# Where ScalarE copies a unit's turned weights: before or behind the next unit's two exponentials

## The reference, cut to what matters

```python
def _diff_attn(q, k, v, lam):
    s = jnp.einsum("bqhcd,bkhcd->bhcqk", q, k, preferred_element_type=jnp.float32) * (ATT_QK_DIM ** -0.5)
    p = jax.nn.softmax(s, axis=-1)
    w = p[:, :, 0] - lam * p[:, :, 1]
    return jnp.einsum("bhqk,bkhd->bqhd", w.astype(v.dtype), v)

def _diff_post(o, g, lam_init):
    o = _rmsnorm(o, g, SUBLN_EPS) * (1.0 - lam_init)
    return o.reshape(o.shape[0], o.shape[1], ATT_HEADS * ATT_V_DIM)
```

## Time and profile before

| what | value |
|---|---|
| median of 3 executions | 3102.07 us (3097.54 to 3107.11) |
| the profiled execution's own time | 3098.69 us |
| its span, first to last instruction | 3097.4 us |
| mean granted TensorE clock | 0.974 of full speed |
| TensorE matmuls busy | 2915.4 us, 94% |
| VectorE busy | 1611.4 us, 52% |
| ScalarE busy | 1076.4 us, 35% |
| GpSimd busy | 315.3 us, 10% |
| exponentials of the differential heads (L1386) | 32, from 2128.0 to 2216.2 us |

### The profile page before, as it was taken

The page is one execution under the profiler, slowest core; times in us unless marked ns, Lnnn a source line. Parts: engine busy times, 40 slices in busy tenths (PEclk is TensorE's granted clock), DMA queues, the critical chain, the costliest instruction groups (busy, mean ns, idle before and its releaser), DMA issues.

```text
span 3097.4 us, 39662 instructions
## 1 busy us (share of the span) xinstructions
PE 2915.4 (94%) x16020; PEld 2281.9 (74%) x16020; DVE 1611.4 (52%) x2496; ACT 1076.4 (35%) x1799; POOL 315.3 (10%) x347
## 2 busy tenths in 40 slices
PE   7989999999999988999899998998799999799998
PEld 4766667888888856767677776776578887678886
DVE  2645544656566655754544445537635555344433
ACT  3245443412222242653422335213442233343222
POOL 1012220200000030221201002000310000110000
PEclk8999999999999999999899999999999999899999
DMA  6212001556565511001222321211025554122222
GB/s 259 89 69 103 8 21 42 173 193 210 166 208 187 163 53 41 15 9 54 93 89 89 103 89 68 92 55 55 21 92 173 170 176 157 56 75 96 95 95 75
DMA packets 88477, 315.73 MB, mean 102 GB/s; under 512 B 9991, under 2 KB 12295, under 8 KB 88040
## 3 DMA queue, kind: packets, MB, share of 16 engines
q1 hardware_dynamic: 59040, 213.94, 20.4%
q10 hardware_dynamic: 29256, 99.26, 9.7%
HBM read 311.06 MB, written 2.10 MB: 101 GB/s over the span
## 4 chain that ended last, share of the span: by engine, by line
PE 87%; DVE 5%; ACT 4%; issue 2%; POOL 1%; DMA 1%; SPq 0%; ACTq 0%; DVEq 0%; POOLq 0%
PE bank L669 43%; PE bank L673 21%; PE bank L1108 4%; PE bank L1125 3%; PE bank L1169 3%; PE bank L2841 1%; PE bank L1947 1%; PE bank L1685 1%; PE bank L1569 1%; PE bank L1117 1%; ACT t L920 1%; ACT t L1207 1%; PE bank L730 1%; PE bank L738 1%; PE bank L2933 1%
## 5 line engine op out<-in xcount | busy, mean ns | idle before, releaser
L669 PE MATMUL bank<-t 128*128 128x512 f32 (+1 forms) x6432 | 1750.3, 372 | 31.2 <-DVE t L2447 11.1
L669 PEld LDWEIGHTS bank<-t 128*128 128x128 f32 x6432 | 1113.4, 189 | 285.1 <-issue 58.9
L673 PE MATMUL bank<-t 128*128 128x512 f32 (+1 forms) x3216 | 1067.7, 371 | 5.3 <-POOL t L929 5.2
L673 PEld LDWEIGHTS bank<-t 128*128 128x128 f32 x3216 | 555.7, 189 | 128.1 <-POOL t L929 11.2
L489 ACT ACTIVATE t<-t 128x1024 fp32r<-128x1024 f32 x350 | 367.6, 1054 | 701.6 <-PE bank L673 459.5
L499 DVE TENSOR_TENSOR t<-t 128x1024 fp32r<-128x1024 f32 x350 | 430.7, 1234 | 336.8 <-ACT t L489 334.9
L686 DVE SCALAR_TENSOR_TENSOR t<-bank,t 128x512 f32<-128x512 f32 x192 | 129.7, 693 | 354.8 <-PE bank L673 337.7
L587 DVE SCALAR_TENSOR_TENSOR t<-t 128x1024 f32<-128x1024 f32 x176 | 210.0, 1219 | 1.8 <-DMA t<-in_mod 1.4
L1024 DVE TENSOR_TENSOR t<-t 128x512 f32<-128x512 f32 (+1 forms) x128 | 98.3, 768 | 182.2 <-ACT t L1000 182.2
L1309 POOL TENSOR_SCALAR t<-t 128x768 f32<-128x768 f32 (+3 forms) x160 | 125.7, 788 | 552.5 <-DVE t L1277 552.5
L1000 ACT ACTIVATE t<-bank 128x512 f32<-128x512 f32 (+1 forms) x128 | 83.1, 650 | 247.1 <-PE bank L673 245.9
(11 more groups left out here) (296 smaller groups left out, 2238.0 us busy)
## 6 DMA issues: line engine op xcount, KB each, us to landing
t<-in_mod ACTq DMA_DIRECT2D x176, 512.0 KB, 4.1
t<-in_l0fc SPq DMA_DIRECT2D x64, 512.0 KB, 4.1
t<-in_l1fc SPq DMA_DIRECT2D x64, 512.0 KB, 3.4
t<-in_s0fc SPq DMA_DIRECT2D x64, 512.0 KB, 4.2
t<-in_s1fc SPq DMA_DIRECT2D x64, 512.0 KB, 3.4
t<-in_mod SPq DMA_DIRECT2D x48, 512.0 KB, 4.5
t<-in_mixin SPq DMA_DIRECT2D x24, 512.0 KB, 3.4
t<-in_l0in SPq DMA_DIRECT2D x12, 512.0 KB, 3.5
```

Source lines behind the costliest of these rows:

```text
L669: pe.matmul(acc.ap[:, o:o + m], w[:, ws], Hh[:, k, o:o + m], start=k == 0 and w is hi, stop=False)
L673: ins = pe.matmul(acc.ap[:, o:o + m], hi[:, ws], Hl[:, k, o:o + m], start=False, stop=k == NK - 1)
```

## The change

In ScalarE's loop the two exponentials of unit u are issued before the copy of the turned unit u - 1, and no longer behind it. Nothing is added or removed, and the other engines' orders stay.

```diff
             def rest(high):
                 for u in range(1, n + 2):
+                    if 2 <= u < n:
+                        early(u)
                     if u <= n:
                         turned(u - 1)
-                    if 2 <= u < n:
-                        early(u)
                     if u >= 2:
                         values(u - 2)
                     if 2 <= u < 6:
```

## The result

| | before | after |
|---|---|---|
| median of 20 executions | 3102.19 us (3097.54 to 3109.41) | 3106.93 us (3102.62 to 3110.09) |
| ratio | 1 | 1.0012 (95%: 1.0006 to 1.0017) |
| the profiled execution, its span | 3098.69, 3097.4 | 3109.56, 3108.2 |

What follows compares the result with a forecast made beforehand. No engine is full; the loop of about 79 us is a ring of waits. Root 1.02 plus head 0.81 gives 1.83 us slower, 3100.5 for the profiled execution, 3103.9 for the median with 3.4 added; range 3098 to 3110.

Steps and rivals of the forecast that it cites:

- The ring and the plain units: Plain units cycle through scores, maximum, two exponentials, scores; the copy is not in it, so moving it there gains 0.
- The slot: ScalarE's time for the copy in its new place behind the exponentials: 0.39 us, upper bound 0.45.
- (a) The root: Units 5, 9, 13: the later square starts GpSimd's root 0.34 us later, all on the path, three times: 1.02 us.
- (b) The head: Units 7, 11, 15: exponentials gain 0.13 us, yet square and head's transposes come 0.27 later, three times: 0.81 us.
- The sum: Root cost 1.02 plus head cost 0.81 makes the loop 1.83 us longer; forecast chance 0.70 for +1.2 to +2.2.
- What follows the stage: Serial dense products on TensorE after the loop: a start 1.8 us later is an end 1.8 us later.
- A: Rival: only one of the root and head costs lands, +0.8 to +1.0 us, 3103.0; chance 0.13.
- B: Rival: the earlier exponentials bring no loss, -0.4 to 0 us, 3101.7 to 3102.1; chance 0.10.
- C: Rival: longer TensorE gaps in units 6 and 7 drop its clock to 1.2 GHz, +19 us, 3121; chance 0.02.

Runs made afterwards that it cites:

- the eight plain units alone: Copy moved behind the exponentials only in units 2, 3, 4, 6, 8, 10, 12 and 14, otherwise the kernel before; stage 78.54 us, ratio 0.9996.
- two more copies behind: Changed kernel with two more copies into an unread table before the moved copy in units 8, 10, 12 and 14; stage 80.59 us, ratio 1.0012.
- the root units' kernel: Copy moved behind the exponentials only in units 5, 9 and 13, otherwise the kernel before; stage 81.04 us, ratio 1.0002.
- the head units alone: Copy moved behind the exponentials only in units 7, 11 and 15, otherwise the kernel before; stage 81.70 us, ratio 1.0004.
- the kernel before with two more copies in front: Kernel before with two more copies in front of the exponentials in units 8, 10, 12 and 14; stage 79.92 us, ratio 1.0013.
- the two partial kernels: Kernel before with the copy moved only in units 5, 9, 13 (stage 81.04 us) or only in units 7, 11, 15 (stage 81.70 us).
- the kernel with four more copies: Changed kernel with four more copies before the moved one in units 5, 7, 9, 11, 13 and 15; stage 91.15 us, ratio 1.0043.
- the kernel with the split root: Kernel before with GpSimd's four scalings of y moved one unit later, behind its scaling of units 6, 10, 14; stage 78.13 us, ratio 1.0000.

## Why the prediction was right, point by point

**The ring and the plain units.** Right. The exponentials there go by the maximum; the eight plain units alone gave 78.54 for 78.53, and two more copies behind cost nothing.

**The slot.** Forecast 0.39, measured 0.37 (2194.00 to 2194.37). The estimate of 0.41 from the Trainium skill's figures (ScalarE: Activation LUTs, What ACT_TABLE_LOAD costs) is 0.04 over the row.

**(a) The root.** Forecast 0.34 three times, 1.02. The steps that hold it grew by 0.59, 0.28 and 0.28 in the root units' kernel, 1.15 (1.18 by its stage), and the copy in (b) is not in that. The mechanism and place were right, the size was 0.13 short, and not evenly. The start of the root came 0.32 later in all three, near the forecast 0.34. Where it waited for the square, its first step L1501 shows 0.77 or 0.78 us in place of 0.19 or 0.20, and the step behind it (L1503) is shorter in return: in the second and third root 1.02 in place of 1.64, so that these roots took 0.05 less in all and 0.28 was left on the path. In the root of head 0 L1503 took 1.35 in place of 1.65, which doesn't make up for it, and from the root's start to GpSimd's next scaling it was 5.00 us (2173.77 to 2178.77) in place of 4.72. That is the extra 0.28 of the first root, the same in all three profiles of after and in the root units' kernel. Why L1503 stayed longer there, the runs don't show.

**(b) The head.** Forecast 0.27 three times, 0.81; the transposes went from 3.55 to 3.81 behind the maximum, 0.26, and the head units alone cost 0.81 without the clock's part.

**The sum.** 1.83 against 1.94 in the stage (1.81 to 2.08 over the pairs of profiles), inside the bounds of 1.2 to 2.2. The median of 3106.93 lies in the stated range of 3098 to 3110, but that says little: the range is mostly the scatter of the runs and would have held a loss of 6 us too. It is the stage that bears out the sum. The forecast of 3103.9 for the median is 3.0 under the measured one, and only part of that is explained, by what follows.

**What follows the stage.** Here the forecast was short by 1.5. The step that failed is "a start that is 1.8 us later is an end that is 1.8 us later". From L2841 to the end the program took 874.6 and 874.4 us in the profiles of before, and 876.1, 876.0 and 875.8 in those of after, 1.5 more. Stretch rows of before and after, over all of it:

```profile
2222.82:3097.40 874.58, 835.10 (x3623) 661.77 (x3621) 396.81 (x497) 278.73 (x364) 36.44 (x38) 0.97 0.34 114
```

```profile
2232.13:3108.20 876.07, 836.88 (x3623) 663.39 (x3621) 396.92 (x497) 278.54 (x364) 36.42 (x38) 0.96 0.34 113
```

The work is the same (3623 matmul rows), and the mean clock 0.97 and 0.96. The same instructions of ScalarE, timed from L2841, show where the 1.5 gathers:

| instruction, us behind L2841 | before, twice | after, three times |
|---|---|---|
| first L824, a copy | 54.17, 54.14 | 54.13, 54.16, 54.15 |
| first L1002, in the dense layers | 76.08, 76.06 | 76.60, 76.56, 76.45 |
| an L824 in front of the pooling layer | 431.29, 431.26 | 431.81, 431.77, 431.66 |
| the second L2097 behind it | 438.63, 438.59 | 440.16, 440.12, 440.00 |

So 0.5 us comes between 54 and 76 us, around the place of low clock at 2280 that the earlier trace rows shows, and 1.0 us between 431 and 438 us. In steps of 50 us from L2841 the granted clock of most is the same in all five profiles; the largest difference is in the ninth, 400 to 450 us, with 0.90 in both of before and 0.86 in all three of after. It is the passage into the pooling layer, where TensorE waits for other engines. Rows of before and of after from 430 us behind L2841 on:

```profile
2652.82:2657.82 5.00, 3.13 (x19) 2.17 (x16) 0.93 (x4) 1.84 (x3) 0.00 (x0) 0.92 0.75 281
2657.82:2662.82 5.00, 0.49 (x3) 0.20 (x1) 3.23 (x5) 3.50 (x5) 1.71 (x2) 0.50 0.05 22
2662.82:2667.82 5.00, 4.02 (x21) 4.05 (x22) 1.52 (x3) 5.00 (x8) 4.60 (x4) 0.55 0.02 3
2667.82:2672.82 5.00, 3.44 (x30) 3.23 (x28) 0.31 (x1) 1.53 (x3) 1.37 (x2) 1.00 0.12 36
```

```profile
2662.13:2667.13 5.00, 2.92 (x12) 1.96 (x12) 0.43 (x3) 1.22 (x4) 0.00 (x0) 0.74 0.73 264
2667.13:2672.13 5.00, 2.07 (x8) 1.78 (x8) 3.01 (x5) 2.79 (x4) 0.28 (x1) 0.50 0.15 65
2672.13:2677.13 5.00, 2.49 (x12) 2.52 (x12) 2.33 (x4) 5.00 (x8) 4.62 (x4) 0.50 0.02 3
2677.13:2682.13 5.00, 5.00 (x38) 4.80 (x37) 0.00 (x0) 1.60 (x3) 2.78 (x3) 0.89 0.00 0
```

In the second row of each the clock is at 0.50. Before, TensorE is busy only 0.49 us in it, so that the low clock costs next to nothing there; after, it is busy 2.07 us in it, and the next row is at 0.50 throughout, where it was 0.55. The first row is at 0.74, where it was 0.92. Counted from L2841, the clock fell sooner and rose later. So the change cost some 1.9 in the stage and 1.5 behind it, 3.4 us, and the three sets of runs say 3.7, 1.6 and 3.1. That the larger part of the excess lies there and goes with a lower clock is shown by five profiles, and two variants bear it out: the plain units alone, whose stage is as long as before (78.54), have 0.90 in the ninth step and 874.6 behind the stage, and the kernel with two more copies behind, whose stage is as long as after (80.59), has 0.86 and 875.9. And the kernel before with two more copies in front, whose order is not changed at all but whose stage is longer (79.92), has 876.5. So the excess came with the longer stage and not with the new order as such. But it is no simple function of the length (a stage of 78.29 us has 875.2 behind it), and why the clock falls at another point of the program is not shown. Nor is it shown why the profiles of after reached the stage at 2149.3 to 2151.7 us and all the others at 2144.3 to 2148.2, with the same program up to there. If those 5 us between the means of after and before were the change's, it would cost over 8 us, which is above the upper ends of all three intervals (5.3, 4.3 and 5.6 us); so most of them must be scatter of single executions.

**The rivals.** A (only one cost lands) is out by the two partial kernels. B (no loss) is out by all. C, the clock, had 0.02 as something that decides, and it did not happen in the changed kernel's stage; but its mechanism was nearer than I had it. I had argued from 72% busy, a mean over the whole stage. The clock fell in the stage in 5 of the 9 kernels that are neither before nor after, each time at the end of it, where a head, two waits and two sets of values follow each other (in the kernel with four more copies also in units 7 and 11), for 1.3 to 2.5 us where it is worked out above. In the 5 us before the fall TensorE was busy 2.9 to 3.3 us in four of them (all but the kernel with four more copies), and in these no wait of TensorE at this end of the stage was over 1.6 us; but the kernel before has 2.73 of 5 us (2212.5 to 2217.5) and the one after 2.48 (2221 to 2226), both at 1.00 and with no fall behind them. So the busy share of such a stretch does not tell them apart, and what does is not shown. In the part behind the stage the clock did cost the changed kernel time. By the Trainium skill (TensorE: Matmul & The Clock Gate, What's actually happening) activity releases the throttle; the trace agrees in so far as in the head units' kernel the clock was back at 1.00 in 2230 to 2231 us, with TensorE busy all of it in the dense matmuls that had begun at 2228.19. In the root units' kernel it was back sooner, at 1.00 in 2227 to 2228 us, before those began.

## What to carry to other kernels

An instruction that is free where it stands is not free one place further back: ask for every instruction that it is put in front of who waits for that, in the few iterations that differ from the plain one (here six of fourteen, a root or a head). The exponentials looked as if they stood behind the copy, but a unit without the copy at hand gave the same 0.99 us from maximum to exponential, so nothing was to be won there. A change of 2 us in a program of 3100 is read from the length of its stage, which repeats to 0.15 us here, and not from medians alone. Look then at the granted clock in the stage and behind it: here it changed a gain or loss of 2 us by as much again.

## What the runs showed of the hardware that was not expected

The granted clock fell to 0.50 in a stage without one long wait, where TensorE had been busy 2.9 to 3.3 of the 5 us before (in four of the cases), in the profiles of 5 of 9 variants, and in none of two of before and three of after. 12 matmuls of 128 x 128 then took 2.7 to 2.9 us in place of 1.6, and the kernel with the split root gave back 2.32 of the 2.72 us that it had won. A stage that is 2 us longer made the part behind it 1.5 us longer, 0.5 of it some 65 us and 1.0 some 435 us behind the stage, where the change touches nothing and where the clock goes to 0.50 in both kernels; so it was in all three profiles. A small instruction of GpSimd that had waited 0.40 us for ScalarE showed 0.77 us in place of 0.19, and yet in two of three roots the step behind it was shorter by as much.
